# Two mixers rebuilt as single stages, another order of heads in a third, and a masked quarter left out of two attentions

## The reference

```python
mask = key_chunk[None, :] <= q_chunk[:, None]            # latent, chunks of 64
causal = (own * MOBA_BLOCK + offs_k)[None, :] <= (qi * Q_BLOCK + offs_q)[:, None]   # hybrid
p = jax.nn.softmax(jnp.where(mask, sc, -jnp.inf), axis=-1)
```

```python
def chunked_sgu(h, w_in, v_norm, w_s, b_s, w_out):       # gating mixer, 8 heads of 256
    z = jax.nn.gelu(h @ w_in)                            # w_in: 1024 x 4096
    u, v = jnp.split(z, 2, axis=-1)
    v = rmsnorm(v, v_norm)                               # over 2048 values of a token
    ws = jnp.where(causal[None], w_s, 0)                 # 8 x 128 x 128
    gate = einsum('hts,bcshd->bcthd', ws, v) + b_s.T     # over tokens, chunks of 128
    return (u * gate) @ w_out                            # w_out: 2048 x 1024

def pool_mixer(h, w_in, w_grp, scale, w_out):            # 4 groups of 256 channels
    groups = split(h @ w_in, 4)
    pooled = [causal_mean(g, w) - g for g, w in zip(groups, (2, 4, 8, 16))]
    y = einsum('bsgc,gcd->bsgd', pooled, w_grp)
    return (y * scale) @ w_out
```

## Time and profile before

| | |
|---|---|
| time, median of 3 runs | 3128.78 us (3128.7 to 3132.61) |
| profiled execution: time, span of the trace | 3136.45 us, 3134.7 us |
| PE, DVE, ACT busy, share of the span | 93%, 58%, 47% |
| granted clock of PE, mean | 0.956 of full speed |
| DMA | 489.30 MB, 155 GB/s read over the span |

### The profile page before, as it was taken

The page is one execution under the profiler, slowest core; times in us unless marked ns, Lnnn a source line. Parts: engine busy times, 40 slices in busy tenths (PEclk is TensorE's granted clock), DMA queues, the critical chain, the costliest instruction groups (busy, mean ns, idle before and its releaser), DMA issues. The chain is left out here.

```text
span 3134.7 us, 47710 instructions
## 1 busy us (share of the span) xinstructions
PE 2923.1 (93%) x20616; PEld 2704.3 (86%) x20616; DVE 1822.2 (58%) x2468; ACT 1467.9 (47%) x1953; POOL 16.3 (1%) x21
## 2 busy tenths in 40 slices
PE   6998788999999799999999999999997999998899
PEld 6998686999997599898999898989987899997798
DVE  4567463656656365545468756556554655655555
ACT  4454212545545354434466544445443544543543
POOL 0000000000000000000000100000000000000000
PEclk9999786999999799999999999999998999999999
DMA  6555100565653155555555245555654455553554
GB/s 196 188 181 164 61 1 9 180 188 159 189 188 110 61 188 188 175 188 168 171 161 176 68 162 184 189 165 175 189 175 134 148 189 188 181 188 116 182 188 134
DMA packets 370038, 489.30 MB, mean 156 GB/s; under 512 B 15183, under 2 KB 329124, under 8 KB 369700
## 3 DMA queue, kind: packets, MB, share of 16 engines
q1 hardware_dynamic: 369232, 486.04, 48.9%
q10 hardware_dynamic: 596, 0.21, 0.0%
HBM read 485.15 MB, written 1.05 MB: 155 GB/s over the span
## 5 line engine op out<-in xcount | busy, mean ns | idle before, releaser
L848 PE MATMUL work<-input_hi,weights_hi 128*128 128x256 f32 x3520 | 990.3, 281 | 8.2 <-DVE weights_lo L230 6.2
L850 PE MATMUL work<-input_lo,weights_hi 128*128 128x256 f32 x3520 | 986.3, 280 | 0.0
L851 PE MATMUL work<-input_hi,weights_lo 128*128 128x256 f32 x3520 | 986.3, 280 | 0.0
L225 DVE TENSOR_TENSOR weights_lo<-weights_raw,weights_hi 128x2048 fp32r<-128x2048 f32 (+2 forms) x282 | 629.4, 2236 | 408.6 <-ACT weights_hi L208 408.6
L848 PEld LDWEIGHTS work<-input_hi,weights_hi 128*128 128x128 f32 x3520 | 665.6, 189 | 13.8 <-DVE weights_lo L230 6.6
L850 PEld LDWEIGHTS work<-input_lo,weights_hi 128*128 128x128 f32 x3520 | 665.5, 189 | 4.4
L851 PEld LDWEIGHTS work<-input_hi,weights_lo 128*128 128x128 f32 x3520 | 665.2, 189 | 0.0
L212 ACT ACTIVATE weights_hi<-weights_raw,params 128x512 fp32r<-128x512 f32 (+2 forms) x736 | 462.4, 702 | 388.0 <-DMA weights_raw<-in_ffn_w_gu 190.2
L208 ACT ACTIVATE weights_hi<-weights_raw 128x2048 fp32r<-128x2048 f32 (+2 forms) x282 | 525.0, 1865 | 180.5 <-DMA weights_raw<-in_ffn_w_up 108.2
L230 DVE SCALAR_TENSOR_TENSOR weights_lo<-weights_raw,params,weights_hi 128x512 fp32r<-128x512 f32 (+2 forms) x736 | 492.8, 733 | 193.3 <-ACT weights_hi L212 193.2
L315 PE MATMUL acc<-weights_hi,hidden_hi 128*128 128x512 f32 x880 | 349.9, 398 | 8.3 <-DVE hidden_lo L950 7.0
(11 more groups left out here) (497 smaller groups left out, 3310.7 us busy)
## 6 DMA issues: line engine op xcount, KB each, us to landing
weights_raw<-in_ffn_w_gu SPq DMA_DIRECT2D x176, 512.0 KB, 4.8
weights_raw<-in_ffn_w_in SPq DMA_DIRECT2D x176, 512.0 KB, 4.8
weights_raw<-in_ffn_w_down SPq DMA_DIRECT2D x66, 1024.0 KB, 4.9
weights_raw<-in_w_in SPq DMA_DIRECT2D x44, 1024.0 KB, 5.3
weights_raw<-in_ffn_w_out SPq DMA_DIRECT2D x44, 1024.0 KB, 4.9
weights_raw<-in_a_w_in SPq DMA_DIRECT2D x29, 1024.0 KB, 5.5
weights_raw<-in_ffn_w_gate SPq DMA_DIRECT2D x44, 512.0 KB, 3.9
weights_raw<-in_ffn_w_up SPq DMA_DIRECT2D x44, 512.0 KB, 4.9
```

The source lines that it names most:

```text
L225: last = self.nc.vector.tensor_tensor(self.wl[:, n % SLOTS, 0:kc * cols], raw, self.wh[:, n % SLOTS, 0:kc * cols].bitcast(F32), ALU.subtract)
L848: nc.tensor.matmul(o, wh[:, k, ms], K.hi[:, c, :], start=(c == 0 and m == 0), stop=False, skip_group_check=True)
L850: nc.tensor.matmul(o, wh[:, k, ms], K.lo[:, c, :], start=False, stop=False, skip_group_check=True)
L851: last = nc.tensor.matmul(o, wl[:, k, ms], K.hi[:, c, :], start=False, stop=(c == DC - 1), skip_group_check=True)
```

## The change

It has four parts. **The latent mixer** keeps its steps but orders them anew: on PE the scores of the head after next stand ahead of a head's transposes, on ACT the exponentials follow suit, one output quarter moves from head 4 to head 5 and one from head 5 to head 6, the last mix stands inside the last two items, and ACT and DVE round and split no item past n0+8 among the heads (n0+10 before). **The masked quarter** is left out in the latent heads and the hybrid attention: scores, mask, probabilities and turned probabilities are 384 wide, in three squares of 128, instead of 512; the maximum takes two DVE instructions instead of one. **The gating mixer** becomes one stage of 24 items: v first, by tokens, its squares by `bn_stats` on DVE while projections run, the spatial weights loaded behind item n0+5, turned after the fifth item and scaled by the inverse root of each token; then per head the projection of u, the gates of the head before, and the output rows of two heads before, items interleaved in the list. The product is rounded and split per head. **The pool mixer** becomes one stage of 12 items: groups in the order 3, 2, 1, 0, the sliding sums of a group behind its projection, the group weights and output rows interleaved. Both take their input straight from the FFN's tail (`Feed`) and join its block.

Everything above the latent mixer stands two lines lower in the new kernel.

```diff
+                            ts, at = tokens[t]
+                            seen = slice(0, (t + 1) * P)
+                            nc.tensor.matmul(K.work[:, h % 2, at], qn[:, h - MH, ts], K.k_nope[:, h - MH, seen], start=True, stop=False)
+                            last = nc.tensor.matmul(K.work[:, h % 2, at], qr[:, h - MH, ts], K.k_rope[:, 0, seen],
+                                                    start=False, stop=True)
...
+                        v = lambda kt: K.v_mla[:, kt, (h - MH) * P:(h - MH + 1) * P]
+                        nc.tensor.matmul(K.work[:, 3, 0:T], v(0), flat(pT, h)[:, 0:2 * P], start=True, stop=False, skip_group_check=True)
+                        last = nc.tensor.matmul(K.work[:, 3, P:T], v(1), flat(pT, h)[:, 2 * P:3 * P], start=False, stop=True,
+                                                skip_group_check=True)
...
                 expand(0)
+                scores(2)
                 turn(0)
-                scores(2)
                 expand(1)
+                scores(3)
+                turn(1)
                 mix(0)
-                turn(1)
-                scores(3)
...
                 scores(4)
+                turn(3)
                 mix(2)
-                turn(3)
-                pe.wait_ge(*rotated(4))
                 scores(5)
                 mix(3)
-                pe.wait_ge(*split(MH))
                 for h in range(MH, HEADS):
-                    for i, q in (((0, 0), (0, 1)), ((0, 2), (0, 3)), (), ((1, 0),), ((1, 1), (1, 2)), ((1, 3),))[h - MH]:
+                    if h + 2 < HEADS:
+                        pe.wait_ge(*rotated(3 if h + 2 < MH + 4 else 4))
+                        scores(h + 2)
+                    for i, q in (((0, 0),), ((0, 1), (0, 2)), ((0, 3),), ((1, 0),), ((1, 1), (1, 2)), ((1, 3),))[h - MH]:
+                        if (i, q) == (0, 0):
+                            pe.wait_ge(*rotated(4))
+                            pe.wait_ge(*split(MH))
                         if (i, q) == (1, 0):
                             pe.wait_ge(*split(MH + 2))
                         out_quarter(i, q)
                     turn(h)
-                    if h + 2 < HEADS:
-                        scores(h + 2)
                     if h > MH:
                         mix(h - 1)
-                mix(HEADS - 1)
 
                 def before(j):
+                    if j == 1:
+                        mix(HEADS - 1)
                     if j in (0, 2):
                         pe.wait_ge(*split(MH + 4 + j))
                 K.last_rows(pe, OI + 2, (pair(2), pair(3)), tail, before)
...
                 for h in range(MH, HEADS):
-                    K.round_weights(act, OI + 3 + h - MH)
+                    K.round_weights(act, OI + 2 + min(h - MH, 3))
                     take(h)
+                    if h + 2 < HEADS:
+                        exps(h + 2)
                     if h > MH:
                         attended(h - 1)
-                    if h + 2 < HEADS:
-                        exps(h + 2)
...
+        with K.stage(24, join=True) as (block, n0):
...
+            UI = [n0 + i for i in (8, 9, 10, 12, 14, 16, 18, 20)]
+            OI = [n0 + i for i in (11, 13, 15, 17, 19, 21, 22, 23)]
...
+                K.load_weights(sp, n0 + SLOTS + 1)
...
+                factors(0)
+                factors(1)
+                gates(0)
+                for h in range(2, GH):
+                    factors(h)
+                    gates(h - 1)
+                    if h == GH - 1:
+                        gates(h)
+                    out_rows(h - 2)
...
+                    if h >= 1:
+                        act.wait_ge(*multiplied(h))
+                        if h >= 4:
+                            act.wait_ge(K.used, OI[h - 4] + 1)
+                        nc.scalar.activation(yhi[:, (h - 1) % 3, :, :], u[:, (h - 1) % 2, :, :], ACT.Copy).then_inc(*rounded.up())
+                    if h < GH:
+                        K.round_weights(act, min(UI[h] + 1 + LEAD, n0 + 24))
+                tail.scalar_part(act)
...
+                    if h < GH:
+                        K.split_weights(dve, min(UI[h] + LEAD, n0 + 24))
+                    if h >= 1:
+                        g = h - 1
+                        dve.wait_ge(*rounded(g + 1))
+                        nc.vector.tensor_tensor(ylo[:, g % 3, :, :], u[:, g % 2, :, :], yhi[:, g % 3, :, :].bitcast(F32),
+                                                ALU.subtract).then_inc(*split.up())
+                    if h < GH:
+                        K.split_weights(dve, min(UI[h] + 1 + LEAD, n0 + 24))
+                tail.vector_part(dve, OI[GH - 1], 1.0, None)
...
+        with K.stage(12, join=True) as (block, n0):
...
+            GI, OI = (n0 + 4, n0 + 5, n0 + 7, n0 + 9), (n0 + 6, n0 + 8, n0 + 10, n0 + 11)
...
+                mix(0)
+                mix(1)
+                feed.await_row(pe)
+                out_rows(0)
+                mix(2)
+                out_rows(1)
+                mix(3)
...
+                for j in range(4):
+                    K.round_weights(act, n0 + j + 1 + LEAD)
+                    act.wait_ge(*ready(j + 1))
+                    nc.scalar.activation(phi[:, 2 * j:2 * j + 2, :], pooled[:, j % 2, :, :], ACT.Copy).then_inc(*rounded.up())
+                for j in range(4):
+                    act.wait_ge(K.used, GI[j] + 1)
+                    for m in range(2):
+                        g = 2 * group(j) + m
+                        last = nc.scalar.activation(K.hi[:, 2 * j + m, :], two(K.work[:, j % 2, :])[:, m, :], ACT.Copy,
+                                                    scale=scale[:, g:g + 1])
+                    last.then_inc(*y_rounded.up())
+                    K.round_weights(act, (n0 + 9, n0 + 10, n0 + 12, n0 + 12)[j])
+                tail.scalar_part(act)
...
+                    K.split_weights(dve, n0 + j + 1 + LEAD)
+                    dve.wait_ge(*rounded(j + 1))
+                    nc.vector.tensor_tensor(plo[:, 2 * j:2 * j + 2, :], pooled[:, j % 2, :, :],
+                                            phi[:, 2 * j:2 * j + 2, :].bitcast(F32), ALU.subtract).then_inc(*split.up())
+                for j in range(4):
...
+                    last.then_inc(*y_split.up())
+                    K.split_weights(dve, (n0 + 9, n0 + 10, n0 + 12, n0 + 12)[j])
+                tail.vector_part(dve, OI[3], 1.0, None)
...
+        plan_columns(K, A["a_w_in_3"][0], 2 * D, 2 * D)
+        plan_columns(K, A["a_w_in_3"][0], 0, 2 * 2 * P)
+        for h in range(2, GH):
+            plan_columns(K, A["a_w_in_3"][0], 2 * P * h, 2 * P)
+            K.rows(A["a_w_out_3"][0], 2 * P * (h - 2), 2)
+        for h in range(GH - 2, GH):
+            K.rows(A["a_w_out_3"][0], 2 * P * h, 2)
...
+        for g in (3, 2, 1, 0):
+            K.columns(A["b_w_in_3"][0], 2 * P * g, 2 * P, DC)
+        grouped = lambda g: K.columns(A["b_w_grp_3"][0, g], 0, 2 * P, 2)
+        grouped(3)
+        for g in (2, 1, 0):
+            grouped(g)
+            K.rows(A["b_w_out_3"][0], 2 * P * (g + 1), 2)
+        K.rows(A["b_w_out_3"][0], 0, 2)
```

428 lines of the change are left out of this document (282 added, 146 removed).

## The result

| | before | after |
|---|---|---|
| time, median (lowest to highest) | 3128.74 us (3125.38 to 3132.61, 4 runs) | 3052.33 us (3050.82 to 3053.95, 4 runs) |
| profiled execution: time, span | 3136.45 us, 3134.7 us | 3053.95 us, 3051.8 us |
| ratio of the times | | 0.9761, 95% interval 0.9746 to 0.9776 |

A forecast was written before the change was run, and what follows sets the result against it. It took PE, busy for 93% of the span, as the bound, other engines mattering only where PE waits. 27 + 4.5 + 25 + 18.5 = 75 us off the 3128.8 us median gave 3054 us, range 3030 to 3084.

The forecast's parts named there:

- 1. Latent mixer: Latent mixer: the load wait, other waits and half clock shrink; 28 us less, taken as 27, ends 13 and 42.
- The load step: Latent mixer: the rounding that waits for item n0+10's load leaves the heads, so PE's 12.6 us wait goes.
- the low end: Latent mixer: lowest gain, 13 us, if only the wait on the load goes.
- 11 us of waits: Latent mixer: PE waits remaining in the new order: 3 before the fourth mix, 1 and 4 at heads 6 and 7, three about 1.
- near 0.10 us for such records: Sign in the new profile: scores records of 128 columns take near 0.10 us.
- 2. Hybrid attention: Hybrid attention: the masked quarter saves PE 0.60 us a head, 4.8 us; taken as 4.5, ends 2 and 5.
- Rival D: Masked quarter saves nothing, 128 columns being paced by weight load; 4.5 and some 3 us fall away: 3061; chance 0.04.
- 3. Gating mixer: Gating mixer: 35.1 us of waits and half clock go, less new waits at start, loop, end, tail: 25 us, ends 15, 33.
- 4. Pool mixer: Pool mixer: last two items come 20.6 us earlier, 2.0 back in the tail: 18.5 us, ends 12 and 25.
- A: Latent, gating and pool mixers: small waits cost more than they measure; gain 53 us, 3075 us; chance 0.20.
- B: Everything stays dense, latent mixer at full clock: 40 + 5 + 31 + 23 = 99 us gained, 3030 us; chance 0.16.
- C: Gating loop and pool: short waits keep PE at 1.2 GHz; 75 - 108 = -33, slower at 3162 us; chance 0.04.

The follow-up runs named there:

- undo_latent: The changed kernel with the latent mixer of before (old order, all roundings between the heads, 512-wide scores): 3082.39 us, ratio 0.9836.
- cap_alone: The kernel before, with ACT and DVE rounding and splitting no item past n0+8 between the latent heads: 3116.17 us, ratio 0.9945.
- undo_hybrid: The changed kernel with the hybrid attention of before (512-wide scores): 3057.67 us, ratio 0.9756.
- latent_full_width: The changed kernel with scores, mask, probabilities and mixes 512 wide again in the latent heads alone: 3054.96 us, ratio 0.9753.
- undo_pool: The changed kernel with the pool mixer of before and its order of items: 3069.4 us, ratio 0.9793.
- gating_loop: The changed kernel with one rounding of an item moved ahead of the product's rounding on ACT in the gating loop: 3042.41 us, ratio 0.9716.
- latent_order: The changed kernel with the latent attended head split before the next softening, rounded before the next exponentials, and one rotation behind it: 3055.38 us, ratio 0.975.

## Why the prediction was right, point by point

**The sum.** 75 us predicted; 76 between the medians, 80.6 between the stages of the two traces. The expected profiled run was 3061, the measured one 3053.95: the profile before was one of its slower executions (the latent mixer 3.5 us longer than its repetition in undo_latent, at a lower clock), and a sum made from its rows carries that along. That the 75 came out so near is in part luck: against the stages the terms were off by +6.8, -0.1, -2.3 and +1.2 us, of which the first, the latent mixer's, is half due to that execution and was in part made good by the third.

**1. Latent mixer, 27 predicted; 33.8 in the traces, 30.3 undone.** The load step was right and under-priced: with half clock it is 17 to 21 us by itself (cap_alone), where the low end had 13. ACT no longer waits for any load in this mixer. Of the stretch behind, the window that answers to the first one of the earlier trace rows is:

```profile
978.54:1040.45 61.91, 57.00 (x262) 40.68 (x261) 42.02 (x94) 30.97 (x79) 0.00 (x0) 0.86 0.19 65
```

67 us were predicted, 61.9 came: 11 us of waits were laid out and 4.9 are there (the one at the fourth mix, 3 predicted, 2.3; the one of 4 at head 7, 2.6; the one at head 6 and the three small ones never came), and half clock costs 57.0 x 0.14 = 8 where 9 was kept. The price of a narrow score was too low. Scores of head 9, 128 columns and then 256:

```profile
1024.36 0.39 PE L2015 MATMUL work<-k_nope,q_nope 128*128 128x128 f32 x2
1024.68 0.48 PE L2016 MATMUL work<-k_rope,q_rope 64*128 64x128 f32 x2
1025.10 0.70 PE L2015 MATMUL work<-k_nope,q_nope 128*128 128x256 f32 x2
```

0.32 and 0.42 us for two records of 128 columns, 0.16 and 0.21 each instead of 0.125; 24 of them are 1.4 us. Of the signs named ahead, near 0.10 us for such records is the one that failed most plainly; what makes these records slower than those of the hybrid attention stays open.

**2. Hybrid attention, 4.5 predicted.** The same rows as the earlier trace rows after:

```profile
1519.77 0.55 PE L2352 MATMUL acc<-const,probs 128*128 128x128 f32 x3 [0.16 <-DVE probs L2487]
1520.15 0.82 PE L2344 MATMUL work<-k_att,q_att 128*128 128x128 f32 x4
1520.81 0.82 PE L2361 MATMUL acc<-probs_turned,v_att 128*128 128x256 f32 x4
```

0.38 for 0.50 and 0.66 for 0.87, the mix likewise: 0.12 + 0.21 + 0.21 = 0.54 us a head, 4.3 in all. The second block gains 4.4 us from before to after and 7 from undo_hybrid to most of the others; what goes beyond 4.3 is clock, most of it some 175 us past the attention (last section). Rival D is refuted, here by the records and in the latent heads by the 2.7 us of latent_full_width.

**3. Gating mixer, 25 predicted; 22.7 in the traces, 21.0 undone with its start.** Each wait came within 0.5 us. What the sum lacked stands behind the waits: the restart of 0.24 us for each of the four, 1 us; and half clock behind the wait of 2.1 us. PE's timeline there:

```profile
2406.57 0.47 PE L317 MATMUL acc<-weights_hi,sgu_out_hi 128*128 128x512 f32 x1 [2.07 <-DVE sgu_out_lo L3230]
2407.34 0.62 PE L317 MATMUL acc<-weights_hi,sgu_out_hi 128*128 128x512 f32 x1
2408.61 0.63 PE L317 MATMUL acc<-weights_hi,sgu_out_hi 128*128 128x512 f32 x1
2410.98 0.39 PE L317 MATMUL acc<-weights_hi,sgu_out_hi 128*128 128x512 f32 x1
```

The matmuls of 0.63 us are at 1.2 GHz, those of 0.39 at 2.4: about 1.5 us. For the pool mixer the prediction had priced such a piece, here it had not.

**4. Pool mixer, 18.5 predicted; 19.7 in the traces, 18.7 undone.** The wait of 5.5 us came as 4.8, the tail's 2.0 as 1.5.

**The rivals.** A fell: waits for ACT and DVE remain in the latent mixer, but at 0.86 of the clock and for 4.9 us. B came true only there, in part (34 of its 40). C, slower, is refuted where it should have shown. The loop of the gating mixer, with its four waits, has this window:

```profile
2347.00:2405.00 58.00, 53.27 (x340) 46.89 (x340) 34.05 (x34) 19.49 (x16) 0.00 (x0) 1.00 0.49 162
```

The granted clock is 1.00. The Trainium skill ("TensorE: Matmul & The Clock Gate", A second HAM failure mode: psum-queue depth-cycling) tells of a kernel in which short idles between groups of matmuls that cycle through PSUM banks made the clock swing. This loop's trace does not agree, with its idles of 1.0 us, 13.3 us apart; behind the later one of 2.1 us it does show a drop.

## What to carry to other kernels

An instruction that waits for a load must not stand in an in-order queue ahead of one that the critical engine needs: ask of every prefetch step which instruction frees its buffer, and whether that one is behind the queue that the step blocks. Price a removed wait with what stands behind it (here 13.9 us of waits took 3.5 to 7 of half clock with them), and a new short wait at its shown length plus the restart. Where two engines in series are the bound, as in the latent mixer, reordering them moves the wait and does little else; where one of them idles ahead of the step, as ACT in the gating loop, one moved line removes it.

## What the runs showed of the hardware

The same instructions, with the same waits, ran at different clocks in different executions. 660 to 680 us behind the latent mixer's end mark, in a stage that no kernel here touches, PE's windows in undo_pool and in gating_loop are:

```profile
1717.48:1737.48 20.00, 17.11 (x159) 16.66 (x160) 13.19 (x17) 12.49 (x12) 2.15 (x2) 1.00 0.33 109
```

```profile
1716.25:1736.25 20.00, 17.81 (x143) 17.20 (x144) 12.31 (x15) 11.54 (x11) 1.81 (x1) 0.83 0.32 107
```

PE's waits in them are equal in both (1.1, 1.1 and 0.7 us), and the clock is 1.00 in one and 0.83 in the other, worth some 3 us. In the profiles the drop is there in all three kernels with the former hybrid attention (before, undo_hybrid, cap_alone) and in two of the eleven with the new one (gating_loop and latent_order). So the narrower attention may make it rarer; what decides it stays open. The changed kernel's own profile has no drop there, but over the 20 us from 180 and from 800 us behind the mark its clock is 0.74 where undo_pool has 0.83. Such differences go with the second block's 1015.7 to 1019.9 us for one and the same code, and are a reason why a few microseconds of a change were visible in its stage and not in the time of the whole.
